# Opening of a fused two-block kernel: features first, modulation by chunk pairs, ten tiles on TensorE and six on VectorE

## What is computed

```python
def rms_norm(x):
    xf = x.astype(jnp.float32)
    return (xf * lax.rsqrt(jnp.mean(xf * xf, axis=-1, keepdims=True) + EPS)).astype(x.dtype)
def modulate(x, shift, scale):
    return rms_norm(x) * (1.0 + scale) + shift
...
    s_lat = jax.nn.silu(c)[:, None, :]
    s_ctx = jax.nn.silu(c_ctx)[None, None, :]
...
        mod_l = jnp.split(s_lat @ ada_w[i] + ada_b[i], ADA_CHUNKS, axis=-1)
        mod_c = jnp.split(s_ctx @ ada_w[i] + ada_b[i], ADA_CHUNKS, axis=-1)
        h_lat = modulate(x_lat, mod_l[0], mod_l[1])
        h_ctx = modulate(x_ctx, mod_c[0], mod_c[1])
...
        q, k, v, g = jnp.split(h @ w_in, splits, axis=-1)
```

## Time and profile before

| what | us |
|---|---|
| median of 3 timed runs (lowest, highest) | 2978.72 (2968.82, 2981.04) |
| the profiled execution, its own time | 2966.58 |
| its span | 2964.8 |
| TensorE busy in the span | 2910.1 |
| VectorE busy | 1977.1 |
| ScalarE busy | 1113.0 |

### The profile page before, as it was taken

One profiled execution on the slowest core, in us unless ns is written; L12 is line 12 of the kernel. 1 busy time (PEld: TensorE's weight loads), 2 busy tenths in 40 slices (PEclk: granted clock), 3 DMA queues, 4 the chain that ended last, 5 costly groups with the idle time before them and its releaser, 6 DMA issues.

```text
span 2964.8 us, 40076 instructions
## 1 busy us (share of the span) xinstructions
PE 2910.1 (98%) x14480; PEld 2363.8 (80%) x14480; DVE 1977.1 (67%) x3088; ACT 1113.0 (38%) x1593; POOL 178.5 (6%) x161
## 2 busy tenths in 40 slices
PE   9999999999999999998999999999999999999998
PEld 7888678888887788866888888688878888876887
DVE  7973688567786788785898746456644622657875
ACT  3232524332243665424341323443344422423443
POOL 1300000000001000000030200000000000002120
PEclk9999999999999999999999999999999999999999
DMA  7663065666633156563366552663265622542554
GB/s 276 228 213 101 13 213 186 200 202 241 206 105 114 59 174 216 171 162 91 107 202 215 189 167 77 234 242 107 96 242 196 220 95 97 161 168 100 200 189 142
DMA packets 131282, 490.70 MB, mean 166 GB/s; under 512 B 15803, under 2 KB 15804, under 8 KB 128948
## 3 DMA queue, kind: packets, MB, share of 16 engines
q1 hardware_dynamic: 125236, 454.89, 46.2%
q0 software_dynamic: 5888, 33.66, 3.1%
HBM read 458.34 MB, written 17.83 MB: 161 GB/s over the span
## 4 chain that ended last, share of the span: by engine, by line
PE 78%; issue 10%; DVE 7%; ACT 2%; DMA 2%; SPq 1%; POOL 0%; DVEq 0%; ACTq 0%; POOLq 0%
PE bank L801 21%; PE bank L803 20%; PE bank L802 20%; PE bank L814 4%; PE bank L815 2%; PE bank L1730 2%; SPq L582 1%; DVE w_lo L2527 1%; PE bank L1112 1%; PE bank L1352 1%; DVE x_res L2653 1%; PE bank L813 1%; DVE x_res L2659 1%; PE bank L1218 1%; PE bank L1501 1%
## 5 line engine op out<-in xcount | busy, mean ns | idle before, releaser
L2527 DVE TENSOR_TENSOR w_lo<-w_raw,w_hi 128x1024 fp32r<-128x1024 f32 x585 | 722.6, 1239 | 577.6 <-ACT w_hi L1798 568.1
L1798 ACT ACTIVATE w_hi<-w_raw 128x1024 fp32r<-128x1024 f32 x588 | 619.1, 1055 | 757.0 <-PE bank L803 632.1
L801 PE MATMUL bank<-h_hi,w_hi 128*128 128x512 f32 (+1 forms) x1432 | 526.3, 368 | 2.1 <-DVE h_lo L3315 1.0
L802 PE MATMUL bank<-h_lo,w_hi 128*128 128x512 f32 (+1 forms) x1432 | 518.7, 362 | 0.0
L803 PE MATMUL bank<-h_hi,w_lo 128*128 128x512 f32 (+1 forms) x1432 | 518.4, 362 | 0.0
L801 PEld LDWEIGHTS bank<-h_hi,w_hi 128*128 128x128 f32 x1432 | 270.4, 189 | 64.8 <-issue 21.0
L802 PEld LDWEIGHTS bank<-h_lo,w_hi 128*128 128x128 f32 x1432 | 270.4, 189 | 42.3 <-issue 1.2
L803 PEld LDWEIGHTS bank<-h_hi,w_lo 128*128 128x128 f32 x1432 | 270.3, 189 | 41.7
L801 PE MATMUL bank<-w_hi,xm_hi 128*128 128x512 f32 x512 | 201.5, 394 | 0.0
L803 PE MATMUL bank<-w_hi,xm_lo 128*128 128x512 f32 x512 | 199.6, 390 | 0.0
L802 PE MATMUL bank<-w_lo,xm_hi 128*128 128x512 f32 x512 | 199.3, 389 | 0.0
(11 more groups left out here) (444 smaller groups left out, 5286.8 us busy)
## 6 DMA issues: line engine op xcount, KB each, us to landing
w_raw<-in_weights SPq DMA_DIRECT2D x620, 512.0 KB, 3.4
ada_ring_f<-in_ada SPq DMA_DIRECT2D x56, 512.0 KB, 4.1
ada_ring_g<-in_ada SPq DMA_DIRECT2D x44, 512.0 KB, 4.3
ada_ring_b<-in_ada SPq DMA_DIRECT2D x38, 512.0 KB, 4.1
ada_ring_a<-in_ada SPq DMA_DIRECT2D x32, 512.0 KB, 3.5
conv_shifted<-conv_in SPq DMA_DIRECT2D x128, 94.0 KB, 3.4
ada_first<-in_ada SPq DMA_DIRECT2D x16, 512.0 KB, 15.2
v_spill<-ml_v POOLq DMA_DIRECT2D x4, 1024.0 KB, 6.4
```

Of the source, the lines that this page charges most:

```text
L801: mm(out, lhs[0], rhs[0], start=start, stop=False)
L802: mm(out, lhs[0], rhs[1], start=False, stop=False)
L1798: return nc.scalar.activation(out, in_, func, **kw)
L2527: V.tensor_tensor(WLO[:, slot, :], RAW[:, slot, :], WHI[:, slot, :].bitcast(F32), SUB)\
```

## The change

- SP loads `X` first, then the modulation tiles in pairs (c, 8 + c), with the first three weight tiles behind the second pair and the fourth behind the last.
- Chunks 3, 5 and 7 (`ADA_VECTOR`) get both their tiles from VectorE, the other five chunks theirs from TensorE: ten tiles.
- TensorE's order: spreading of the vectors, 6 fillers, four ones-matmuls (VectorE adds the squares in twos first), then pairs 0, 1, 2 with 3 fillers behind each, then the chunks of the projection; pair 4 stands behind chunk 1 and pair 6 behind chunk 3 (`after_chunk`).
- VectorE scales `X` by the inverse root of the mean square without the modulation (`first_scaled`, one instruction over 512 tokens), and finishes the modulation of one chunk at a time (`first_mods`); ScalarE applies scale and shift of each stream (`first_features`) and copies the result into the high part; VectorE's low part is one instruction over 512.
- The fourth spread vector is passed through silu behind the squares; the table for the root is loaded by a small instruction ahead of it.
- The load of the rotary table waits for the fourth chunk's low part.
- On the host the ten tiles for TensorE are laid out as the seven were; two shared semaphores get new offsets.

```diff
@@ -105,7 +105,7 @@
-ADA_TENSOR = (3, 5, 7, 9, 11, 13, 15)
+ADA_VECTOR = (3, 5, 7)
...
@@ -530,12 +531,14 @@
             sp.dma_start(ONE_ROW, consts_d[1][0:1, :]).then_inc(S("c_rows_in"), 16)
-            for n in range(ADA_FIRST):
-                sp.dma_start(ADA_RAW[:, n, :], ada[n]).then_inc(S(f"ada_first{n // 2}"), 16)
-                if n == 5:
-                    sp.dma_start(X[:, :, :], x_t).then_inc(S("x_first"), 16)
-            for s in range(SLOTS):
-                sp.dma_start(RAW[:, s, :], weights[s]).then_inc(raw_full[s], 16)
+            sp.dma_start(X[:, :, :], x_t).then_inc(S("x_first"), 16)
+            for c in range(DC):
+                if c == 2:
+                    for s in range(LOOKAHEAD):
+                        sp.dma_start(RAW[:, s, :], weights[s]).then_inc(raw_full[s], 16)
+                for n in (c, DC + c):
+                    sp.dma_start(ADA_RAW[:, n, :], ada[n]).then_inc(S(f"ada_first{c}"), 16)
+            sp.dma_start(RAW[:, LOOKAHEAD, :], weights[LOOKAHEAD]).then_inc(raw_full[LOOKAHEAD], 16)
             sp.dma_start(C_ROWS[:, 2:4, :], c_rows_d[:, 2:4, :]).then_inc(S("c_rows2_in"), 16)
...
@@ -678,7 +681,7 @@
-            pool.wait_ge(S("raw_done"), 1)
+            pool.wait_ge(S("h_lo_done"), 4)
             pool.dma_start(ROPE[:, :, :, :], ret_rope_d).then_inc(S("vecs_in"), 16)
...
@@ -975,6 +978,8 @@
                             last.then_inc(S("tile_done"), 1)
+                    if after_chunk is not None:
+                        after_chunk(k)
                 for s in range(ahead, body):
...
@@ -1045,23 +1050,32 @@
                     .then_inc(S("c_spread"), 1)
-            pe.wait_ge(S("silu_c_done"), 2)
-            for n in ADA_TENSOR:
-                if n == 7:
-                    pe.wait_ge(S("consts_in"), 32)
-                if n >= 7:
-                    for c in {7: (0, 1), 9: (2, 3), 11: (4, 5), 13: (6, 7), 15: ()}[n]:
-                        pe.wait_ge(S("sq_done"), c + 1)
-                        mm(PS[0][:, :], ONES[:, :], FIRST_SQ[:, c, :], start=c == 0, stop=c == DC - 1)\
-                            .then_inc(S("sq_used"), 1)
-                pe.wait_ge(S(f"ada_first{n // 2}"), 16 * 2)
-                for k in range(DC):
-                    last = mm(PS[7][:, 2 * n:2 * n + 2], ADA_RAW[:, n, k * P:(k + 1) * P], vec("c_cols", 2 * k, 2),
-                              start=k == 0, stop=k == DC - 1)
-            last.then_inc(S("ada_pe_done"), 1)
-            turn_over(5, 6)
-            pe.wait_ge(S("std_done"), 1)
-            gemm_rows("ret_qk", TOK, 0, ["qk_free"], 16, lows_by_chunk=True)
+            pe.wait_ge(S("consts_in"), 32)
+            pe.wait_ge(S("silu_c_done"), 1)
+            turn_over(6, 3)
+            for i in range(DC // 2):
+                pe.wait_ge(S("first_sum"), N("first_sum", i + 1))
+                last = mm(PS[0][:, :], ONES[:, :], FIRST_SQ[:, 2 * i, :], start=i == 0, stop=i == DC // 2 - 1)
+            last.then_inc(S("sq_used"), DC)
+
+            def first_mods(c):
+
+                if c in ADA_VECTOR:
+                    return
+                pe.wait_ge(S(f"ada_first{c}"), 16 * 2)
+                if c == 0:
+                    pe.wait_ge(S("silu_c_done"), 2)
+                for half in range(2):
+                    for k in range(DC):
+                        last = mm(PS[4 + c % 4][:, 2 * half:2 * half + 2], ADA_RAW[:, DC * half + c, k * P:(k + 1) * P],
+                                  vec("c_cols", 2 * k, 2), start=k == 0, stop=k == DC - 1)
+                last.then_inc(S("ada_pe_done"), 1)
+
+            for c in range(3):
+                first_mods(c)
+                turn_over(3, 3)
+            gemm_rows("ret_qk", TOK, 0, ["qk_free"], 16, lows_by_chunk=True,
+                      after_chunk=lambda k: first_mods(k + 3) if k + 3 < DC else None)
             def rv_copied(n):
...
@@ -1941,19 +1955,36 @@
             f(CELL[0:1, 0:1], ONE_ROW[:, 0:1], ACT.Silu)
-            for b in range(4):
+            def c_row(b):
                 act.wait_ge(S("c_spread"), b + 1)
-                last = f(C_ROWS[:, b // 2, b % 2 * 512:b % 2 * 512 + 512], PS[1 + b][:, :], ACT.Silu)
-            last.then_inc(S("silu_c_done"), 1)
+                return f(C_ROWS[:, b // 2, b % 2 * 512:b % 2 * 512 + 512], PS[1 + b][:, :], ACT.Silu)
+
+            for b in range(3):
+                c_row(b)
             act.wait_ge(S("vecs_in"), 16)
             f(vec("c_cols", 0, 2 * DC), vec("c_cols", 0, 2 * DC), ACT.Silu).then_inc(S("silu_c_done"), 1)
             act.wait_ge(S("x_first"), 16)
             for c in range(DC):
                 f(FIRST_SQ[:, c, :], X[:, c, :], ACT.Square).then_inc(S("sq_done"), 1)
+            c_row(3).then_inc(S("silu_c_done"), 1)
+            f(CELL[:, 1:2], vec("eps", 0), ACT.Sqrt)
             std(0, TOK, 0)
-            for n in range(LOOKAHEAD):
-                hi(n, n, first=True)
-            h_hi(0, TOK, shifts(0, 0))
+
+            def first_features(c):
+
+                act.wait_ge(S("raw_done"), c + 1)
+                if c >= 4:
+                    act.wait_ge(S("h_lo_done"), c - 3)
+                for st, cols in STREAMS:
+                    own(f(hbuf(c)[:, cols], FIRST_SQ[:, c, cols], ACT.Identity, scale=mod(0, 1, c, st), bias=mod(0, 0, c, st)))
+                f(HHI[:, c, :], hbuf(c), ACT.Copy).then_inc(S("h_hi_done"), 1)
+
+            hi(0, 0, first=True)
+            hi(1, 1, first=True)
+            first_features(0)
+            hi(2, 2, first=True)
+            for c in range(1, DC):
+                first_features(c)
             hi_ahead("ret_qk", 0, 0)
...
@@ -2796,21 +2827,37 @@
-            dve.wait_ge(S("silu_c_done"), 1)
-            for n in range(ADA_FIRST):
-                if n in ADA_TENSOR:
-                    continue
-                dve.wait_ge(S(f"ada_first{n // 2}"), 16 * 2)
-                own(ada_product(n, ADA_RAW[:, n, :], AREA_A))
+            dve.wait_ge(S("vecs_in"), 16)
+            FIRST_B = FUSE[:, 0:2 * DC]
+            own(V.tensor_copy(FIRST_B[:, 0:DC], vec("ada_b", 0, DC)))
+            own(V.tensor_scalar(FIRST_B[:, DC:2 * DC], vec("ada_b", DC, DC), 1.0, None, ADD))
+            dve.wait_ge(S("x_first"), 16)
+            for i in range(DC // 2):
+                dve.wait_ge(S("sq_done"), 2 * i + 2)
+                V.tensor_tensor(FIRST_SQ[:, 2 * i, :], FIRST_SQ[:, 2 * i, :], FIRST_SQ[:, 2 * i + 1, :], ADD)\
+                    .then_inc(S("first_sum"), 1)
             inverse_std(0, TOK)
-            dve.wait_ge(S("ada_pe_done"), N("ada_pe_done", 1))
-
-            def every_other(x):
-                return x[:, 4:2 * ADA_FIRST].rearrange("p (a b) -> p a b", b=4)[:, :, 2:4]
-            own(V.tensor_copy(every_other(MOD), every_other(PS[7])))
-            dve.wait_ge(S("vecs_in"), 16)
-            ada_finish(0, ADA_FIRST)
-            dve.wait_ge(S("x_first"), 16)
+
+            def first_scaled(c):
+
+                own(V.tensor_tensor(FIRST_SQ[:, c, :], X[:, c, :], tmp(2), MUL))
+
+            def first_product(c, half):
+
+                dve.wait_ge(S(f"ada_first{c}"), 16 * 2)
+                dve.wait_ge(S("silu_c_done"), 2)
+                own(ada_product(DC * half + c, ADA_RAW[:, DC * half + c, :], AREA_A))
+
+            def first_mods(c):
+
+                mods = MOD[:, 0:4 * DC].rearrange("p (h a t) -> p h a t", h=2, t=2)[:, :, c, :]
+                bias = FIRST_B.rearrange("p (h a) -> p h a", h=2)[:, :, c].unsqueeze(2).broadcast_to([P, 2, 2])
+                if c in ADA_VECTOR:
+                    products = mods
+                else:
+                    dve.wait_ge(S("ada_pe_done"), N("ada_pe_done", c + 1 - sum(v < c for v in ADA_VECTOR)))
+                    products = PS[4 + c % 4][:, 0:4].rearrange("p (h t) -> p h t", t=2)
+                V.tensor_tensor(mods, products, bias, ADD).then_inc(S("raw_done"), 1)
...
@@ -2820,7 +2867,18 @@
                     last.then_inc(S("w_lo_done"), LOOKAHEAD)
-            modulate(0, TOK, *mods(0, 0), weight_low=first_low)
+            first_scaled(0)
+            first_mods(0)
+            for c in range(DC):
+                if c < DC - 1:
+                    first_scaled(c + 1)
+                    first_mods(c + 1)
+                first_low(c)
+                dve.wait_ge(S("h_hi_done"), c + 1)
+                V.tensor_tensor(HLO[:, c, :], hbuf(c), HHI[:, c, :].bitcast(F32), SUB).then_inc(S("h_lo_done"), 1)
+                for half, early in ((0, 3), (1, 2)):
+                    if c + early in ADA_VECTOR:
+                        first_product(c + early, half)
...
@@ -3963,7 +4021,7 @@
-    for n in ADA_TENSOR:
+    for n in (n for n in range(ADA_FIRST) if n % DC not in ADA_VECTOR):
         ada[n] = a["ada_w"][0][:, n * P:(n + 1) * P].reshape(DC, P, P).transpose(1, 0, 2).reshape(P, D)
     c_rows = np.broadcast_to(np.stack([a["c"][0], a["c_ctx"], a["c_2"][0], a["c_ctx_2"]])[None], (P, 4, D))
```

(7 more changed lines are left out.)

## The result

| what | before | after |
|---|---|---|
| median of 20 runs each on one chip (lowest, highest) | 2968.98 (2966.81, 2981.04) | 2979.69 (2973.84, 2986.68) |
| mean of these runs | 2973.30 | 2980.03 |
| the profiled execution, its own time | 2966.58 | 2978.40 |
| its span | 2964.8 | 2976.6 |
| start of tile 3 | 57.81 | 69.73 |

The ratio of the means is 1.0023, with a 95% interval from 1.0012 to 1.0033: slower by 6.7 us, within the 0.5% that the prediction counts as no change. Between the two profiles the span grew by 11.8 us and the start of tile 3 moved by 11.9. So all of the shift arises in the opening, and none behind it.

A forecast was written before the change was run, and what follows sets the result against it. TensorE's matmul queue was taken to bound the kernel; its opening terms summed to tile 3 at 71.7 against 57.8, +13.9 us, which on a median of 2978.7 gave 2992.6 us, range 2974 to 3004.

The forecast's parts named there:

- Rival C: TensorE's opening: clock stays high from the ones-matmuls on, chunks wait for VectorE; tile 3 at 60.5, +2.7 us, 2981.4; chance 0.18.
- +13.9: Forecast shift in us of the start of tile 3, from 57.8 to 71.7, carried unchanged to the end.
- ones-matmuls end, pair 0 starts: TensorE's opening: spreading ends at 9.84, six fillers are done at 14.8, four ones-matmuls at 18.7.
- pair 0 and its fillers: TensorE ahead of the first chunk: pair passes at the high clock, to 22.4, its fillers to 23.8.
- pair 1 and its fillers: TensorE: clock falls 2.6 us into the pair, which takes 4.65 us, to 28.4; fillers low, to 31.2.
- pair 2 and its fillers: TensorE: pair wholly at the low clock, to 38.2; its fillers end at 41.0.
- pair 4: TensorE behind chunk 1: the clock falls 2.6 us into the pair, which takes 4.65 us, to 50.5.
- pair 6: TensorE behind chunk 3: the clock falls 2.6 us into the pair, which takes 4.65 us, to 61.4.
- rival B: TensorE's opening: clock falls already in pair 0; tile 3 at 76.4, +18.6 us, 2997.3; chance 0.32.
- A: The forecast itself: clock falls in pair 1, not pair 0; +13.9 us, between +5.4 and +16.2; chance 0.46.
- lies in the shade of these loads: Opening of the kernel before: loads end last ahead of the projection's first matmul at 40.83, hiding TensorE's share of the modulation.
- the late rise: TensorE's clock rising 5.5 us after a wide run starts, everywhere, in place of 4.35; gives +16.2 us.

The follow-up runs named there:

- e4: The changed kernel with TensorE's modulation matmuls 128 columns wide in place of 2; 2970.96 us.
- e9: The changed kernel, unedited, profiled once more; 2982.11 us.
- e9b: The changed kernel, unedited, profiled a third time; 2980.86 us.
- e1: The kernel before, unedited, profiled once more; 2981.83 us.
- e1b: The kernel before, unedited, profiled again for a second chance at the other group of times; 2967.94 us.
- e2: The kernel before with two more fillers ahead of its first ones-matmul; mean ratio to before 0.9982.
- e5: The changed kernel with 128-column modulation matmuls and without the nine fillers between pairs; 2966.60 us, ratio to before 0.9980.
- e6: The kernel before with its seven TensorE modulation tiles as 128-column matmuls; 2967.17 us, ratio to before 0.9981.

## Why the prediction was wrong, and where it was right

**Right: the view.** The effect is the shift of tile 3, and the shift of tile 3 is the shift of the end (11.9 and 11.8 us). TensorE sets it, the loads do not, VectorE waits for no pair's load, and the clock falls in or behind the narrow pairs. Rival C's schedule appeared as soon as the clock was held (e4).

**Nearly right: the sum.** +13.9 was forecast for tile 3, and 11.9 measured between the profiles; with e9 and e9b in place of after it is 17.0 and 14.2. Against the profiled execution of before the forecast was 2980.5; the profiled executions of after took 2978.40, 2982.11 and 2980.86. By terms:

| step | forecast us | profile of after |
|---|---|---|
| ones-matmuls end, pair 0 starts | 18.7 | 19.95 |
| pair 0 and its fillers | 5.1 | 6.15 (19.95 to 26.10) |
| pair 1 and its fillers | 7.4 | 6.26 |
| pair 2 and its fillers | 9.8 | 9.04 (to 41.40) |
| chunks 0 and 1 | 4.85 | 5.51 (to 46.91) |
| pair 4 | 4.65 | 3.49 |
| chunks 2 and 3 | 6.25 | 5.82 |
| pair 6 | 4.65 | 3.49 |
| chunks 4 to 7 | 10.3 | 10.02 |
| tile 3 | 71.7 | 69.73 |

Three kinds of terms missed. The fillers started at 11.08 and not at 9.84, because they wait for `ones` and `ident`. The fall came behind pair 0, and pair 1 still passed mostly high, because the fillers between the two raised the clock again at 26.9, 3.5 us after they began; this rise I had not foreseen. Behind pairs 4 and 6 the fall came after the pair and not 2.6 us into it, which saved 1.2 us each time. These errors cancel to 2 us, which is luck: e9 shows how loose the terms are, for in that execution the clock falls in pair 0, as in rival B (tile 3 at 76.4 forecast, 74.80 measured). A and B are not alternatives for the kernel; its executions take one or the other, or something between (e9b, 72.04).

**The step that failed: "that execution is 12.1 below the median of the three runs, so for the median I write 2978.7 + 13.9".** That took the 12.1 us for scatter which both kernels share and which a shift carries along. The runs showed a second kind of execution of before alone. Of its 95 timed runs on the chips used here, 52 lie between 2966.42 and 2970.59 (mean 2967.93) and 43 between 2978.66 and 2982.45 (mean 2979.88). e1 is one of the upper ones: its opening is low up to the first chunk, and tile 3 starts at 71.07 instead of 57.22 in e1b, 13.9 us later, as much as the spans differ. The profile that I added to was of the lower group, the median of the three runs of the upper. In after, six fillers and four ones-matmuls stand in one wide run from 11.08 to 19.95, the clock rises in it in all three profiles, and there is no such second group. So the change costs 11.9 us against the lower group and nothing against the upper one: 2967.93 + 11.9 = 2979.8, for a mean of 2980.03. Against the mean of before it is 11.9 less what the upper group adds to that mean, 9 of 20 times 11.5, or 5.2 us: 6.7, as measured. The prediction put +13.9 on a median of the upper group, where the shift is about nothing. The reading behind it, that TensorE's share of the modulation "lies in the shade of these loads", holds for the lower group alone.

The three times shown ahead of the prediction, 2968.82, 2978.72 and 2981.04, held a hint of this, and so did the price of the first ones-matmuls, 3.38 against 1.96: in the profiled execution the clock rose only near the end of that run. An event that a run brings about so narrowly should have been given a chance of not happening.

**The chances.** Slower by over 0.5% had 0.48, because the late rise and B were added to a wrong base; the change came out 0.23% slower, in the class that had 0.49.

## What to carry to other kernels

When a few runs differ by much more than repeated runs do, find out which of them the profile is of, before a shift worked out on that profile is added to a median. Keep matmuls of two columns from standing in long runs on TensorE: 128 columns for the same stationary operand cost 0.1 us more for 32 records and made the kernel 9.1 us faster (e4). A clock that only just rises in a profile can stay low in other executions; two fillers that make the wide run longer settled it here (e2).

## What the runs showed of the hardware

- TensorE at 100% busy can lose its clock: behind 2.3 us of narrow matmuls in e9 (at 21.0), behind 3.5 in after (at 23.5), while 10.88 us of matmuls with 128 columns kept it (e5). The Trainium skill (TensorE: Matmul & The Clock Gate, section "Part 1: The HAM clock gate") lets the clock fall when the engine idles; the wait of 3.35 us in e6 agrees, these falls do not.
- The fall can come when the narrow run is over: in after at 61.06, 1.35 us into the wide matmuls of the projection that follow pair 6 at 59.71, and these matmuls paid (0.43 us each instead of 0.23).
- Executions of one program differ in their first clock rise. By the lengths of the records it comes in the narrow tile from 21.98 to 24.02 in e1b, and not before the first chunk of the projection, from 53.90 on, in e1; tile 3 differs by 13.9 us.
- The granted clock that the trace records reads 1.00 ahead of its first recorded change, whatever the durations say (3.75 us for four records in e1 where 1.96 is the price at the high level).
